# Strictly causal mask of the stick-breaking heads: made by GpSimd selections on the sigmoids instead of a TensorE product on the logits

## The reference, cut to what matters

```python
logits = einsum('bhtd,bhsd->bhts', qh[start:end], kh[:end])
causal = arange(end)[None, :] < (start + arange(128))[:, None]      # strict
log_remain = where(causal, log_sigmoid(-logits), 0.0)
log_after = cumsum(log_remain, reverse=True) - log_remain
weights = where(causal, exp(log_sigmoid(logits) + log_after), 0.0)
out = einsum('bhts,bhsd->bhtd', weights, vh[:end])
```

## Time and profile before

| | us |
|---|---|
| median of 3 runs (lowest, highest) | 1755.6 (1753.77, 1755.68) |
| the profiled execution | 1750.28 |
| its span | 1748.5 |
| TensorE matmul busy in the span | 1465.7 (84%) |
| weight loads / VectorE / ScalarE / GpSimd busy | 786.2 / 503.0 / 374.6 / 278.9 |
| mean granted TensorE clock | 0.914 |

### The profile page before, as it was taken

How to read it: one execution, slowest core, us unless ns; L and a number is a source line. 1 busy time by engine, 2 the same in 40 slices (tenths; PEclk the granted TensorE clock), 3 DMA queues, 4 the chain that set the end, 5 groups by cost and what they waited for, 6 DMA issues and landing times. The chain is left out here.

```text
span 1748.5 us, 17418 instructions
## 1 busy us (share of the span) xinstructions
PE 1465.7 (84%) x6018; PEld 786.2 (45%) x6018; DVE 503.0 (29%) x654; ACT 374.6 (21%) x666; POOL 278.9 (16%) x386
## 2 busy tenths in 40 slices
PE   7999998799899999965889377777787787848997
PEld 4557744344477778742455332222232322314443
DVE  4222034214035555533221411111111111112332
ACT  2221222100135565531221001000100100022221
POOL 1000002100124444421110111111111111100110
PEclk9999998889969999987999589898998989878999
DMA  5211057324002111136111249999999999961220
GB/s 185 72 61 49 1 183 197 92 81 113 1 1 61 30 30 30 30 112 262 60 60 42 109 181 420 389 406 404 408 415 395 397 402 397 399 271 71 79 78 36
DMA packets 106386, 306.41 MB, mean 175 GB/s; under 512 B 22368, under 2 KB 60912, under 8 KB 80368
## 3 DMA queue, kind: packets, MB, share of 16 engines
q1 hardware_dynamic: 96848, 289.16, 44.1%
q0 software_dynamic: 9504, 16.80, 2.6%
HBM read 283.85 MB, written 39.90 MB: 185 GB/s over the span
## 5 line engine op out<-in xcount | busy, mean ns | idle before, releaser
L1463 PE MATMUL pe_gu<-w_gu,xT 128*64 128x512 f32 x1024 | 273.2, 695 | 105.3 <-DMA w_gu<-in_w_expert_up 101.8
L253 PE MATMUL ps<-hT,gst 128*128 128x512 f32 x640 | 281.8, 600 | 2.7 <-DVE hT L410 2.7
L1463 PEld LDWEIGHTS pe_gu<-w_gu,xT 128*64 128x64 f32 x1024 | 83.7, 158 | 272.9 <-issue 271.2
L253 PEld LDWEIGHTS ps<-hT,gst 128*128 128x128 f32 x640 | 122.3, 193 | 151.8 <-issue 150.3
L808 DVE TENSOR_TENSOR_SCAN Pm<-rem,Pm 128x128 f32<-128x128 f32 (+3 forms) x96 | 114.4, 1192 | 115.1 <-ACT brk L749 115.1
L1556 DVE TENSOR_TENSOR hs<-sg,pe_gu 128x256 f32<-128x256 f32 x32 | 13.5, 421 | 378.7 <-ACT sg L1527 378.7
L1131 PE MATMUL p_x<-w_o,mT 128*128 128x512 f32 x256 | 119.0, 620 | 2.4 <-DVE mx L1086 1.3
L1481 PE MATMUL pe_y<-w_d,hTe 128*64 128x512 f32 x512 | 115.4, 592 | 1.1 <-DVE ys L1561 1.1
L1784 PE MATMUL f_pg<-w_gu,f_xT 128*128 128x512 f32 x256 | 114.7, 602 | 1.1 <-ACT f_xT L1702 1.1
L871 POOL TENSOR_TENSOR wt<-brk,Pm 128x128 f32<-128x128 f32 (+3 forms) x96 | 86.0, 896 | 176.1 <-DVE Pm L808 176.1
L267 PE MATMUL psk<-w_tok,hT 128*128 128x260 f32 (+1 forms) x384 | 111.7, 453 | 0.0
(11 more groups left out here) (269 smaller groups left out, 1538.1 us busy)
## 6 DMA issues: line engine op xcount, KB each, us to landing
w_gu<-in_w_expert_gate SPq DMA_DIRECT2D x64, 1024.0 KB
w_gu<-in_w_expert_up SPq DMA_DIRECT2D x64, 1024.0 KB
w_d<-in_w_expert_down SPq DMA_DIRECT2D x64, 1024.0 KB
gst<-in_w_in SPq DMA_DIRECT2D x20, 512.0 KB, 4.3
y_sb<-y_d SPq DMA_DIRECT2D x8, 1024.0 KB, 5.3
qkv_d<-y_sb SPq DMA_DIRECT2D x12, 512.0 KB, 2.6
qk_st<-rows_d SPq DMA_DIRECT2D x8, 768.0 KB, 7.5
gst<-qkv_d SPq DMA_DIRECT2D x8, 768.0 KB, 6.0
```

Of the source, the lines that this page charges most:

```text
L253: last = pe.matmul(ps[s][:, c], w_ct[:, s, k, :], hT[:, k, c], start=k == 0, stop=k == KT - 1)
L1463: last = pe.matmul(p_gu[e * CAP:(e + 1) * CAP, :], xT[:, s, k, e * CAP:(e + 1) * CAP], wv[:, e, :, k, :], start=k == 0, stop=k == KT - 1)
```

## The change

TensorE's product L632 goes, with `negb`, `identb`, their four instructions at the start, and the wait for them. GpSimd instead runs `strict(i, k)` for each of the 8 diagonal strips of a head: two `affine_select` over the strip's last 128 columns, in place, first on `rem` (fill 1.0), then on `brk` (fill 0.0). VectorE's scan of a diagonal strip waits for the first, and GpSimd's own product for the second. In GpSimd's list the selections of strip k+1 are written ahead of the product of strip k.

```diff
-                    diag = c1 == (t + 1) * P
-                    last = pe.matmul(LB[k % 2][:, 0:c1 - c0], qk_st[:, s, 0, t * P:(t + 1) * P], qk_st[:, s, 1, c0:c1],
-                                     start=True, stop=not diag)
-                    if diag:
-                        last = pe.matmul(LB[k % 2][:, c1 - c0 - P:c1 - c0], identb[:], negb[:], start=False, stop=True)
-                    last.then_inc(log_done, 1)
+                    pe.matmul(LB[k % 2][:, 0:c1 - c0], qk_st[:, s, 0, t * P:(t + 1) * P], qk_st[:, s, 1, c0:c1],
+                              start=True, stop=True).then_inc(log_done, 1)
...
-                pe.wait_ge(pool_step, 4)
...
+                    if c1 == (t + 1) * P:
+                        dve.wait_ge(cut_done, i * NT + t + 1)
...
+                def strict(i, k):
+                    t, c0, c1 = STRIPS[k]
+                    d = slice(c1 - c0 - P, c1 - c0)
+                    pool.wait_ge(sig_done, i * NS + (k + 3))
+                    pool.sem_inc(passed, 1)
+                    pool.affine_select(out=rem[:, k % 2, d], in_=rem[:, k % 2, d], compare_op=ALU.is_gt, fill=1.0, base=0,
+                                       pattern=[[-1, P]], channel_multiplier=1).then_inc(cut_done, 1)
+                    pool.affine_select(out=brk[:, k % 2, d], in_=brk[:, k % 2, d], compare_op=ALU.is_gt, fill=0.0, base=0,
+                                       pattern=[[-1, P]], channel_multiplier=1).then_inc(brk_done, 1)
...
+                    pool.wait_ge(brk_done, i * NT + (t + 1))
...
                     for k in range(NS):
+                        if k == 0:
+                            strict(i, 0)
                         if k == NS - 1 and not last:
                             begin(i + 1)
+                        if k < NS - 1 and STRIPS[k + 1][2] == (STRIPS[k + 1][0] + 1) * P:
+                            strict(i, k + 1)
                         if k == 1:
                             pool.wait_ge(ds_done, i + 1)
```

More of the change, by code:

```diff
@@ L567, in stage_mixers @@
         wT = sb("wT", [P, 2, 512])
-        negb = sb("negb", [P, P], BF16)
-        identb = sb("identb", [P, P], BF16)
         LB = [pb(f"LB{i}", [P, 512]) for i in range(2)]
@@ L577, in stage_mixers @@
         passed = sem("passed")
-        pool_step = sem("pool_step")
+        cut_done, brk_done = sem("cut_done"), sem("brk_done")
         qk_done, vt_done, kt_done, xt_done, XT_ok = (sem(n) for n in ("qk_done", "vt_done", "kt_done", "xt_done", "XT_ok"))
```

## The result

| | before | after |
|---|---|---|
| median of 4 runs, us | 1754.83 (1753.77 to 1755.68) | 1815.87 (1813.49 to 1821.17) |
| ratio, 95% interval | | 1.0352, 1.0328 to 1.0377 |
| the profiled execution's span | 1748.5 | 1813.3 |
| mean granted clock | 0.914 | 0.900 |
| GpSimd busy / instructions | 278.9 us / 386 | 340.3 us / 510 |

The change costs 61 us. The forecast was slower, 1781 us, in a range to 1812: the direction was right, the size more than twice too small, and the time lies above the range.

A forecast was written before the change was run, and what follows sets the result against it. The prediction took TensorE's dense list in the mixing stage as the bound. Its terms, 4 x 3.55 + 3 x 3.85 - 0.5 = 25.3 us on 1755.6, gave 1781 us, range 1768 to 1812.

The forecast's parts named there:

- TensorE's list sets the stage, and the first strips have no room: Mixing stage: TensorE streams without waits; GpSimd's products of strips 1 and 2 have 1.9 and 0.2 us spare.
- GpSimd's order makes a loop over one strip: GpSimd's list: product k waits for sigmoids k+1, which wait for product k-1; a two-strip loop becomes a one-strip loop.
- The sum of the loop, 3.55 to 3.85 us a head: Heads 1 to 7: odd heads 3.55 us longer, heads 2, 4 and 6 3.85 us longer.
- where I had written 0.3: From strip 5 on: one selection, 0.3 us, added for strip 10, whose scan stands ahead of the state update's needs.
- a microsecond or more: From strip 5 on: every second strip has no selection, and the products have this much time to spare.
- the wait at strip 1: Head 5, L640 of strip 1: TensorE waits 1.7 us and L640 starts 1.50 us later.
- The price of a selection, 0.30 us: GpSimd, mixing stage: each 128x128 float32 selection takes 0.30 us, bounds 0.16 and 0.5, a pair 0.6.
- one hand-over from ScalarE to GpSimd: Chain of head 5: 0.1 us taken for each hand-over between engines.
- The clock stays at 1.00: Heads 2 to 7, main case: clock 1.00 despite TensorE waits under 2 us; stalls as summed, 55%, 1781 us.
- the rival: Mixing stage: clock falls in TensorE's waits, 2 to 18 us each, 10 taken; 1800 to 1811 us, all seven 1851; 30%.
- L632 gives 3.9 us: TensorE, seven heads at full clock: removing eight L632 products a head, 0.07 us each, saves 3.9 us.
- Head 0 gains 0.5 us: Head 0, at half clock: +0.7 for a wait, -0.8 for L632, -0.4 for the stage's start, together -0.5 us.

The follow-up runs named there:

- gap_short: The kernel before with two extra 512-column selections on GpSimd, into an unread tile, between scan and product of strip 2 in each head: 1793.0 us, ratio 1.0241.
- own_order: The changed kernel with each pair of selections right ahead of its own strip's product, not ahead of the previous strip's: 1768.9 us, ratio 1.0107.
- filled: The changed kernel with two extra 128x128 by 512 TensorE products ahead of its wait for the products of strips 1 and 2: 1802.6 us, ratio 1.0283.
- no_mask: The changed kernel without selections, so without any causal mask on the diagonal blocks: 2256.6 us, only the mixing stage comparable, heads 34.8 us.
- gap_long: The kernel before with four extra 512-column selections on GpSimd, into an unread tile, between scan and product of strip 2: 1788.4 us, ratio 1.0217.
- scan_after: The changed kernel with VectorE's scan of each strip waiting until GpSimd's product of the strip before has ended: 1838.9 us, ratio 1.0500.
- load_only: The kernel before, mask still by TensorE, with two selections per diagonal strip into an unread tile, ahead of the strip's product: 1756.6 us, ratio 1.0018.

## Why the prediction was wrong, point by point

- **TensorE's list sets the stage, and the first strips have no room.** Right: a 1.9 us wait put at one of those places, with all else as before, cost 40 us (gap_short), 13 of them the wait itself.
- **GpSimd's order makes a loop over one strip.** Right, link by link, and shown: with the selections ahead of their own strip's product 47 of 61 us are gone (own_order).
- **The sum of the loop, 3.55 to 3.85 us a head.** This is the first step that failed: its terms for GpSimd's two-input products and `qe` were too small, and at full clock the sum is 7.5 (filled). In head 4 L634 of strip 2 stands 671.53 - 657.98 = 13.55 us into the head and stood 8.0 us in before: +5.5 in place of +3.6. I took the durations of the products and of `qe` from the earlier trace rows, where almost none of them ran beside a scan. The new order puts a scan beside each: 0.36 + 0.62 + 0.89 = 1.9 us. The Trainium skill had the rule (GPSIMD Engine Reference, 8. Key points: contention with VectorE instructions that have two SBUF inputs; section 7, which the prediction names beside it, doesn't say this). I applied it to the selections, which measured 294 ns all the same in this kernel, and not to the two-input products. The trace agrees with the rule for those products. The other 2 us a head come after strip 5, where I had written 0.3: each product there also meets a scan (the products of strips 9 and 10 take 3.49 us together) and the room of "a microsecond or more" was not there. In one place agreement was luck: the wait at strip 1 was forecast at 1.7 us and measured 1.73, but in head 5 L634 of strip 1 was 2.3 us late and not 1.5, with 0.34 us already waited at strip 0.

The forms of the changed kernel (busy us, mean ns), to be held against own_order's above (the 512 columns take 1496 ns here):

```profile
L867 POOL TENSOR_TENSOR wt<-brk,Pm 128x384 f32<-128x384 f32 x16 | 21.0, 1312 | 0.0
...
L889 POOL TENSOR_TENSOR qe<-gst,row_q 128x512 f32<-128x512 f32 x8 | 15.1, 1893 | 0.0
```

- **The price of a selection, 0.30 us.** Right (294 ns); one hand-over from ScalarE to GpSimd is 0.22, not 0.1, three times per chain.
- **The clock stays at 1.00.** This is the second step that failed, and it was the likeliest case only by 55 to 30. It fell in seven heads of seven. The bound of about 3 us in the Trainium skill (TensorE: Matmul & The Clock Gate, Why this matters for your kernels) does not hold here: in five heads of the changed kernel the clock fell with the end of a 1.73 us wait, and in gap_short after one of 1.9 us. Nor is that the least. Now and then it fell for 3.4 us after less: 0.5 us behind the 1.32 us wait in head 2 of own_order, and in head 5 of filled behind waits of 0.69 and 0.33 us, while in other heads of filled it stayed at 1.00 through the same waits. Its price, though, was over-rated in the rival: 13 us in this kernel, 2 a head, not 10, since a low clock runs down in part while TensorE would wait.
- **L632 gives 3.9 us.** Too much: about 1 us (no_mask). The 0.07 us from start to start was read rightly, but the products behind L632 take 0.05 us longer without it.
- **Head 0 gains 0.5 us.** It gained 4 us, by a clock that came back 10 us sooner. That this is the change's doing isn't shown: the low stretch at the start of the stage is 17, 20, 24, 27 or 37 us long in these kernels, and it is 37 in gap_short and 24 in gap_long, which differ by two selections.

Left open: what decides whether the clock falls after a wait of about 1 us, and whether a fall lasts 3.4 or 20 us with the same instructions; and how much of scan_after's loss is clock. An estimate from the two prices above (0.24 and 0.43 us for each us at the low clock) for its 41 us more at the low clock is 10 to 18 us, of the 17 us that its heads 1 to 7 lost against the changed kernel's.

## What to carry to other kernels

A selection or any small operation is cheap on an idle engine, but its place in an in-order list is not: work of strip k+1 written ahead of work of strip k makes strip k wait for the next strip's inputs, and with two buffers that closes a loop. Write such an operation directly ahead of its own consumer, and check for every engine how late each result may be, not how busy the engine is. Before adding waits to a dense TensorE list, count with a fallen clock as well: it fell every time behind a single wait of 1.9 us, and sometimes behind waits of about 1 us; unneeded products in the wait can be cheaper than the wait alone.

## What the runs showed of the hardware

- A GpSimd product with two inputs and a VectorE scan at the same time: the scan keeps its 1.02 or 1.29 us, the product takes 1.76 in place of 0.87 us when it starts later. A one-input 128-column selection kept its 0.29 us where the scan began no sooner than the second of its pair (the changed kernel, own_order), but took 0.57 us on average in load_only, where the scans did not wait for it and it read another tile; one of 512 columns took 1.04 in place of 0.64 in gap_short.
- One 1.9 us wait per head in a dense TensorE stretch brought the clock from 1.00 to 0.50 each of seven times. It stayed there for 3.4, 6.8, 13.7 or 20.5 us.
- Unneeded products in a wait can pay: 3.1 us waits, 1788.4 us; the same with 1.9 us of products in each, 1771.7 us.
- A bf16 product of 128x128 (L632) in a dense list cost 0.02 us: the next product starts 0.07 us later, and the one after it 0.02.
